# Grouping a chunk's matmuls by weight part, and dropping a wait between neighbouring banks, in a one-core two-block transformer kernel

## The reference, cut to what matters

```python
h = _modulate(_rms_norm(x, norm1_g[l]), shift1, scale1)
proj = jnp.einsum("bsd,de->bse", h, w_in[l])
lru_x, lru_gate, q, k, v, g_a, g_b = jnp.split(proj, split_idx, axis=-1)
xc = _causal_depthwise_conv(lru_x, conv_w[l], conv_b[l])
rec = _rg_lru(xc, ...)
...
h2 = _modulate(_rms_norm(x, norm2_g[l]), shift2, scale2)
ff = jnp.square(jax.nn.relu(jnp.einsum("bsd,df->bsf", h2, w_ff1[l])))
x = x + gate2[:, None, :] * jnp.einsum("bsf,fd->bsd", ff, w_ff2[l])
```

## Time and profile before

| | |
|---|---|
| median of three runs | 2824.6 us |
| the profiled execution: its time, its span | 2823.6 us, 2821.7 us |
| TensorE (PE) busy | 2682.9 us, 95% |
| VectorE (DVE) busy | 1995.2 us, 71% |
| ScalarE (ACT) busy | 1449.4 us, 51% |
| mean granted TensorE clock | 0.98 |

### The profile page before, as it was taken

One profiled execution on the slowest core, in us unless ns is written; L12 is line 12 of the kernel. 1 busy time (PEld: TensorE's weight loads), 2 busy tenths in 40 slices (PEclk: granted clock), 3 DMA queues, 4 the chain that ended last, 5 costly groups with the idle time before them and its releaser, 6 DMA issues.

```text
span 2821.7 us, 40822 instructions
## 1 busy us (share of the span) xinstructions
PE 2682.9 (95%) x16090; PEld 2348.0 (83%) x16090; DVE 1995.2 (71%) x2806; ACT 1449.4 (51%) x2167; POOL 141.1 (5%) x177
## 2 busy tenths in 40 slices
PE   4769989999999999999999999999999999999996
PEld 4758778888888788888888888888988888889885
DVE  7967888887798976665666667666466766664666
ACT  3335566655544555555555555544554455445543
POOL 0000000000000000000000010100000121000002
PEclk8979999999999999999999999999999999999998
DMA  8945577787888886666665655665545556665453
GB/s 333 374 150 159 165 232 254 238 271 257 283 302 314 274 283 197 188 189 192 182 199 187 192 174 185 176 183 180 157 143 181 199 165 182 184 175 158 143 175 108
DMA packets 162110, 584.12 MB, mean 207 GB/s; under 512 B 19040, under 2 KB 20320, under 8 KB 161792
## 3 DMA queue, kind: packets, MB, share of 16 engines
q1 hardware_dynamic: 157104, 566.86, 62.0%
q0 software_dynamic: 4528, 12.43, 1.6%
q10 hardware_dynamic: 288, 2.23, 0.2%
HBM read 574.05 MB, written 2.15 MB: 204 GB/s over the span
## 4 chain that ended last, share of the span: by engine, by line
PE 82%; DVE 12%; ACT 4%; issue 1%; DMA 0%; ACTq 0%; SPq 0%; DVEq 0%
PE bank L726 46%; PE bank L728 23%; DVE wlo L1356 3%; DVE raw L1397 3%; PE bank L698 2%; PE bank L700 2%; PE bank L699 2%; PE pO L777 1%; ACT whi L971 1%; PE pS L754 1%; DVE TG L1484 1%; PE pT L766 1%; DVE XC L1817 1%; PE pS L807 1%; DVE bank L1803 1%
## 5 line engine op out<-in xcount | busy, mean ns | idle before, releaser
L726 PE MATMUL bank<-H,whi 128*128 128x512 f32 x4000 | 1424.8, 400 | 8.5 <-DVE wlo L1356 3.9
L1356 DVE TENSOR_TENSOR wlo<-raw,whi 128x1024 fp32r<-128x1024 f32 (+1 forms) x880 | 1075.0, 1233 | 450.3 <-ACT whi L971 447.2
L971 ACT ACTIVATE whi<-raw 128x1024 fp32r<-128x1024 f32 (+1 forms) x880 | 912.1, 1048 | 437.9 <-PE bank L728 350.2
L728 PE MATMUL bank<-H,wlo 128*128 128x256 f32 x4000 | 1122.7, 281 | 0.0
L726 PEld LDWEIGHTS bank<-H,whi 128*128 128x128 f32 x4000 | 752.8, 188 | 196.0 <-DVE wlo L1356 9.0
L728 PEld LDWEIGHTS bank<-H,wlo 128*128 128x128 f32 x4000 | 758.1, 190 | 0.6
L726 PE MATMUL bank<-F,whi 128*128 128x512 f32 x1024 | 355.3, 391 | 0.0
L728 PE MATMUL bank<-F,wlo 128*128 128x256 f32 x1024 | 286.7, 280 | 0.0
L1397 DVE SCALAR_TENSOR_TENSOR raw<-raw,CR 128x1024 f32<-128x1024 f32 x192 | 230.6, 1215 | 0.0
L726 PEld LDWEIGHTS bank<-F,whi 128*128 128x128 f32 x1024 | 191.5, 187 | 42.0
L728 PEld LDWEIGHTS bank<-F,wlo 128*128 128x128 f32 x1024 | 193.6, 189 | 0.0
(11 more groups left out here) (306 smaller groups left out, 3205.5 us busy)
## 6 DMA issues: line engine op xcount, KB each, us to landing
raw<-in_w_in SPq DMA_DIRECT2D x424, 512.0 KB, 4.2
raw<-in_w_ff SPq DMA_DIRECT2D x256, 512.0 KB, 4.3
raw<-in_ada SPq DMA_DIRECT2D x192, 512.0 KB, 5.2
raw<-in_w_out SPq DMA_DIRECT2D x96, 512.0 KB, 4.6
raw<-in_w_lru_out SPq DMA_DIRECT2D x32, 512.0 KB, 4.7
raw<-in_w_attn_out SPq DMA_DIRECT2D x32, 512.0 KB, 5.2
raw<-in_w_kv SPq DMA_DIRECT2D x32, 512.0 KB, 4.5
BT<-gtab POOLq DMA_DIRECT2D x32, 128.0 KB, 4.3
```

The lines of the kernel that those rows point to most:

```text
L726: pe.matmul(o.rearrange("p (a s) -> p a s", a=2), whi[:, s, at_:at_ + 128], both[:, :, kt, :], start=(c == 0 and k == 0), stop=False, skip ...
L728: ins = pe.matmul(high, wlo[:, s, at_:at_ + 128], xh[:, kt, :], start=False, stop=(c == un.nkc - 1 and k == 3), skip_group_check=True)
L971: act.activation(whi[:, s, 0:el.n], raw[el.slot][:, 0:el.n], ACT.Copy).then_inc(s_hi, 1)
L1356: dve.tensor_tensor(wlo[:, s, 0:n], raw[el.slot][:, 0:n], v32(whi[:, s, 0:n]), ALU.subtract).then_inc(s_lo, 1)
```

## The change

Two things. In `products_wide` a chunk's eight matmuls with high weights now come first, block by block with the two halves next to each other (so that the two banks alternate), and its eight with low weights after them; the first eight wait for the high weights (`s_hi`), and the wait on `s_lo` stands between the two groups. In `_plan` a unit that is opened and closed in parts gets no `after`.

```diff
@@ -271,7 +271,7 @@
             if un.mode == "f":
                 un.wide = n_wide
                 n_wide += 1
-        un.after = holder.get(un.bank // 2, ())
+            un.after = holder.get(un.bank // 2, ())
         if un.part in ("", "close"):
@@ -710,22 +710,27 @@
             ch = un.chunks[c]
             s = ch % NSP
+            xh, _, both = tensors[un.x]
+            out = [banks[un.bank + i] for i in range(2)]
+            pe.wait_ge(s_hi, split_no[order[ch]])
+            for k in range(4):
+                kt = 4 * un.corder[c] + k
+                if begins[un.x] is un:
+                    pe.wait_ge(*ready[un.x](kt))
+                for i in range(2):
+                    at_ = k * 256 + i * 128
+                    pe.matmul(out[i].rearrange("p (a s) -> p a s", a=2), whi[:, s, at_:at_ + 128], both[:, :, kt, :],
+                              start=(c == 0 and k == 0), stop=False, skip_group_check=True)
             pe.wait_ge(s_lo, split_no[order[ch]])
-            xh, _, both = tensors[un.x]
-            low_first = un.x in ("Y0", "Y1")
-            for i in range(2):
-                o = banks[un.bank + i]
-                high = o[:, 256:512] if low_first else o[:, 0:256]
-                for k in range(4):
-                    kt = 4 * un.corder[c] + k
-                    if begins[un.x] is un and i == 0:
-                        pe.wait_ge(*ready[un.x](kt))
+            high = slice(256, 512) if un.x in ("Y0", "Y1") else slice(0, 256)
+            for k in range(4):
+                kt = 4 * un.corder[c] + k
+                for i in range(2):
                     at_ = k * 256 + i * 128
-                    pe.matmul(o.rearrange("p (a s) -> p a s", a=2), whi[:, s, at_:at_ + 128], both[:, :, kt, :],
-                              start=(c == 0 and k == 0), stop=False, skip_group_check=True)
-                    ins = pe.matmul(high, wlo[:, s, at_:at_ + 128], xh[:, kt, :], start=False,
+                    ins = pe.matmul(out[i][:, high], wlo[:, s, at_:at_ + 128], xh[:, kt, :], start=False,
                                     stop=(c == un.nkc - 1 and k == 3), skip_group_check=True)
             ins.then_inc(s_mm, 1)
```

## The result

The changed kernel takes 2793.9 us (median of four runs, 2793.3 to 2798.4), against 2831.3 us for the kernel before in the same comparison (2823.8 to 2839.2): a ratio of 0.987, 95% interval 0.983 to 0.991. The forecast was 2788 us in 2770 to 2816, and faster by over 0.5%: that is how it came out. The profiled execution has 2798.4 us and a span of 2796.2, 25.5 less than the 2821.7 before.

What follows compares the result with a forecast made beforehand. It took waits between TensorE and VectorE to bound the kernel ahead of 372 us, and matmul distance from 380 us on. Terms 25 + 2 + 9 = 36 us off 2823.6 gave a forecast of 2788 us, range 2770 to 2816.

Steps and rivals of the forecast that it cites:

- The neighbour's wait: Closing units: with the wait gone VectorE is late at 3.99 us a unit, ending at 188.0 us; gain 22 us.
- what is left is 3.99 - 2.88 = 1.1 us between units: Closing units: TensorE's idle times of 4 to 5 us shrink to 1.1 us, so the clock stays full.
- The first `q` unit: With the low weights' wait in mid-chunk, it would be done near 189.0 us against 216.07, 27 us earlier.
- Whether the gates' loop follows TensorE's 27 us or VectorE's 22: Left unread for the loop after the first q unit; 25 us taken up to 205 us, ends 14 and 28.
- The moved wait from 380 us on: From 380 us on, waiting for low weights in mid-chunk gives back 2 us, ends 0 and 6.
- The distances: Matmul to matmul: no change in feed-forward, 6.6 ns a pair recoverable elsewhere; 9 us taken, bounds 0 and 22.
- A chunk is 2773 ns in any order: Feed-forward: eight high at 226.7 and eight low at 120.0 ns make 2773 ns, as now; no change there.
- The 6.6 ns as a rhythm that alternating lengths fall into: Outside feed-forward: pairs take up to 353.3 instead of 346.7 ns, read as a rhythm that low runs never show.
- Exposed weight loads: Rival, 15%: each low run pays 24 ns a chunk for weight loads, 18 us over 772 chunks; 2816 us.
- Clock at half in the closing units: Rival, 12%: TensorE stays at half clock there, gaining 14 us instead of 25; 2800 to 2809 us.
- High after high at 241: Rival, 8%: high matmuls in succession take 241 ns instead of 227, 112 ns more a chunk; 2884 us.
- Nothing passed on: Rival, 5%: the gates' loop starts by something other than TensorE or VectorE, so 2815 to 2825 us.

Runs made afterwards that it cites:

- after: The changed kernel, with the neighbour's wait dropped and high and low matmuls grouped, against the kernel before: 2793.9 us, ratio 0.987.
- before: The kernel without the change, in the same comparison as the changed one: 2831.3 us.
- runs of sixteen: Changed kernel with every other chunk turned round, low matmuls first: 2792.3 us, 0.987 of the kernel before.
- the longer runs: Changed kernel with the high matmuls of two chunks first, then the low ones of both: 2841.7 us, 1.003 of the kernel before.
- run 113: Not a follow-up run or kernel: 113 is a distance in ns between low matmuls behind a run of high ones, in the changed kernel's feed-forward.
- runs of two: Changed kernel with two high, then two low matmuls in each block, low weights awaited at the chunk's head: 2788.4 us, 0.986 of the kernel before.

## Why the prediction was right, and where it was wrong

**The neighbour's wait: right in size, with one step wrong.** VectorE is late, at the 3.99 us a unit that was forecast, the clock is up at 0.99, and the eighth unit's subtraction ends near 188.8 (four of them lie in the 4.62 us from 187.64), with 188.0 forecast. Forecast 22 us, measured alone 22 to 23.5. What was wrong is "what is left is 3.99 - 2.88 = 1.1 us between units": TensorE has no idle time between the closing units at all, since nothing there makes it wait for VectorE. The full clock came as forecast, but not behind the small idle times from which I argued for it.

**The first `q` unit: right.** Forecast near 190, measured 190.06. The moved wait's part of that is 2.0 to 2.5 us; as a sum for everything up to 205 us, 25 was forecast, and 25.6 is there at the 1000th matmul, 23.1 at the 1500th. The stretch that VectorE leads ends near 348 us, with 345 forecast. "Whether the gates' loop follows TensorE's 27 us or VectorE's 22" has two answers. With the wait at the head, TensorE is 2 us later and the lead at the 1500th matmul is the same, so in *after* the loop follows VectorE. With one tap less, VectorE is 8 us earlier and the lead grows by 3 only, what TensorE gained. The loop follows whichever comes last, and the two are 3 us apart.

**The moved wait from 380 us on: at the low end.** 2 us were forecast with 0 to 6. The matmuls' waits of 2.1 us are gone, but in the time over the whole nothing of it is shown.

**The distances: the term that failed.** "A chunk is 2773 ns in any order" is wrong. The settled distances came out as worked out from the rows, 226.7 and 120.0, but the step from them to a chunk left out the turn from low to high. I had called over 231 ns between high ones the point at which the prediction is wrong, and it is 230.6 in the mean of a run's seven, 227 at its end: just short of it. In feed-forward that is 20 ns x 256 chunks = 5 us lost where 0 was forecast. Outside it a slow chunk went over from 2826.7 to 2793.3 ns, 33 ns, where the forecast had 53 for the chunks that gain at all. That brought 5 us between the 1500th and the 5000th matmul. In the second kind of layer *before* has the slow rhythm in 149 of 257 wide chunks (1692 to 2730 us), the fast one in 39, and the rest stand between attention's jobs: by 33 ns gained and 20 lost some 4 us. But the profiled *after* has two stretches of 3.4 us at half clock there, at 1743 and at 2306 us, that the profiled *before* doesn't have; each costs it about 1.5 us, and what is left between the 9000th and the 16000th matmul is 1.4 us. In the sum, 11 us were forecast for the moved wait and the distances, and 25.2 - 23.1 = 2.1 came; with the 2 us by which the first stages fell short that is what separates 36 from 25.

**Where luck helped.** The medians of the result differ by 37 us, close to the 36 forecast. That agreement is luck: half of the four runs of *before* in that comparison were of its slower group, which I didn't know of. Between the faster groups (*before* near 2824, *after* 2793.3 to 2793.9) it is some 30 us, and the forecast of 2788 us was 6 us too low.

**What I hadn't seen.** "The 6.6 ns as a rhythm that alternating lengths fall into" held better than I had used it: feed-forward itself falls into it in part of the executions (29 of the 76 lie in the slower group), for 14 us. The profile before happened to show the fast one. Against the slower group the grouping gains 14 us more, and the ratio of 0.987 is between the two. With three runs shown I took their median, 2824.6, for the kernel's; it is 2831 in the comparison of the result, and 2824 to 2831 where more were run, by how many fall into the slow rhythm. The forecast time doesn't hang on that, the gain does.

**The rivals.** Exposed weight loads: refuted, since low to low is 120.0 and high to high settles at 227, not 230; the loss on a turn is smaller (20 ns a chunk against 24) but so near to that rival's that the time of a chunk alone would hardly have told them apart. The runs of sixteen do: with 3.4 ns at each of fifteen low matmuls in two chunks they would have stayed near 2798, and they have 2783.3. Clock at half in the closing units: refuted by 0.99. High after high at 241: refuted; 226.7 to 236. Nothing passed on: refuted by the 5000th matmul, 28.5 us earlier. The rule in the Trainium skill, "TensorE: Matmul & The Clock Gate", section "Back-to-back issue gap": its isolated distance of 109 ns for 256 columns doesn't appear; even runs of sixteen have 120.0 here.

**What stays open.** Which resource makes the turn cost what it does, and what tips the alternation into 346.7 or 353.3. The bank order is excluded, and so is one price for a turn at every length. Whether the operands' placement or the moment at which the stage starts decides the rhythm wasn't tried. One coincidence stands in the three profiles that alternate: *before*, with the fast rhythm in feed-forward, has a stretch of 3.4 us at half clock near its start (at 990 us), and the two with the slow rhythm have one of 6.8 us there (at 991 and 965 us). Three executions don't show that one causes the other.

## What to carry to other kernels

When a wait goes, work out what is late next from the pace of the other engine, and then once more what is late behind that: here 20 us of TensorE's waiting were worth 22 to 23.5 us, while the next 8 us taken from VectorE were worth 3. Distances read from two pure streams don't add up to the cost of a mixed one: a change of length has a price of its own, which a kernel with the actual order has to show. And a holding time counts as much as an order: the longer runs that were right for TensorE kept the slots so long that the kernel came out 43 us slower than the one with shorter runs.

## What the runs showed of the hardware

- Matmuls of 512 and 256 moving columns in strict alternation have two rhythms at the full clock, 346.7 and 353.3 ns a pair. The feed-forward stage of some 700 us keeps the one it has in all three profiles, and which it is differs between executions of one program: 13.7 us of 2824.
- In uniform runs, each matmul with its own 128 columns of weights, they settle at 226.7 and 120.0 ns, that is their columns at 2.4 GHz and 13.3 ns. Behind a low run the first five high ones take 228 to 236, and the first two low ones behind a high run 113 and 119.
- The turn costs 3 ns with runs of two, 17 with four, and 20 with eight and with sixteen alike. So runs of two (2787 ns a chunk) are nearly as good as runs of sixteen (2783), and both are better than four or eight (2807, 2793).
- Whether two neighbouring matmuls write one bank or two makes no difference here: 2793.3 ns a chunk in both orders.
